# The first FFN's up product as seven half-size products of summed quarters, on one core

## The reference

```
def _ffn_sublayer(x, shift, scale, gate, pre_g, post_g, w_gu, w_down):
    h = _modulate(_rmsnorm(x, pre_g), shift, scale)
    a, b = jnp.split(h @ w_gu, 2, axis=-1)          # 1024 -> 2 x 2816
    y = (jax.nn.silu(a) * b) @ w_down               # 2816 -> 1024
    return x + FFN_RES_WEIGHT * gate * _rmsnorm(y, post_g)
```

## Time and profile before

| | |
|---|---|
| median of 3 runs | 1954.67 us (1954.18 to 1955.05) |
| span of the profiled execution | 1951.0 us (no other time of it is shown) |
| TensorE busy in the span | 1907.6 us |
| VectorE, ScalarE, GpSimd busy | 1031.5, 820.3, 297.9 us |
| up and down parts of the first FFN, from the third block | 57.79 to 540.66 us |

### The profile page before, as it was taken

How to read it: one execution, slowest core, us unless ns; L and a number is a source line. 1 busy time by engine, 2 the same in 40 slices (tenths; PEclk the granted TensorE clock), 3 DMA queues, 4 the chain that set the end, 5 groups by cost and what they waited for, 6 DMA issues and landing times.

```text
span 1951.0 us, 30914 instructions
## 1 busy us (share of the span) xinstructions
PE 1907.6 (98%) x11473; PEld 1757.5 (90%) x11473; DVE 1031.5 (53%) x1746; ACT 820.3 (42%) x1480; POOL 297.9 (15%) x274
## 2 busy tenths in 40 slices
PE   8999999999998999999999999999999999999997
PEld 5999999999997789999999999997888988888887
DVE  7655433443357665466667766676333543233336
ACT  6322222212247655566556655675222552222223
POOL 0000000000000220153455336540000000000000
PEclk9999999999999999999999999999999999999999
DMA  8333333334221430011111110111223412222232
GB/s 332 119 127 122 128 130 129 125 123 128 80 84 52 146 109 1 3 59 49 35 44 51 49 59 22 48 44 44 97 97 103 156 34 97 97 96 96 95 98 79
DMA packets 50130, 174.83 MB, mean 90 GB/s; under 512 B 6788, under 2 KB 8964, under 8 KB 49808
## 3 DMA queue, kind: packets, MB, share of 16 engines
q1 hardware_dynamic: 38720, 129.95, 20.0%
q0 software_dynamic: 11344, 43.97, 7.1%
HBM read 167.03 MB, written 4.24 MB: 88 GB/s over the span
## 4 chain that ended last, share of the span: by engine, by line
PE 86%; ACT 5%; DVE 5%; issue 2%; DMA 1%; SPq 0%; ACTq 0%; DVEq 0%
PE ps L1862 78%; PE ps L1866 4%; PE ps L2252 1%; PE ps L2176 1%; DMA raw<-W 1%; DVE d_os L1762 1%; DVE d_c L1630 1%; PE ps L2206 1%; ACT w_hi L568 1%; PE ps L2308 1%; DVE w_lo L1162 1%; ACT L981 0%; ACT d_t L966 0%; DVE m_prod L1416 0%; ACT c_u L669 0%
## 5 line engine op out<-in xcount | busy, mean ns | idle before, releaser
L568 ACT ACTIVATE w_hi<-raw 128x1024 fp32r<-128x1024 f32 x193 | 204.6, 1060 | 715.5 <-PE ps L1862 715.2
L1162 DVE TENSOR_TENSOR w_lo<-raw,w_hi 128x1024 fp32r<-128x1024 f32 (+1 forms) x193 | 235.1, 1218 | 405.3 <-ACT w_hi L568 405.1
L1862 PE MATMUL ps<-h_hi,w_hi 128*128 128x384 f32 (+2 forms) x1376 | 407.6, 354 | 7.3 <-DVE h_lo L1231 3.0
L1862 PE MATMUL ps<-h_lo,w_hi 128*128 128x384 f32 (+2 forms) x1376 | 403.4, 348 | 0.0
L1862 PE MATMUL ps<-h_hi,w_lo 128*128 128x384 f32 (+2 forms) x1376 | 394.4, 346 | 0.0
L1862 PEld LDWEIGHTS ps<-h_hi,w_hi 128*128 128x128 f32 x1376 | 248.3, 188 | 27.8 <-DVE h_lo L1231 6.6
L1862 PEld LDWEIGHTS ps<-h_hi,w_lo 128*128 128x128 f32 x1376 | 251.4, 188 | 13.5
L1862 PEld LDWEIGHTS ps<-h_lo,w_hi 128*128 128x128 f32 x1376 | 251.5, 188 | 12.9 <-issue 1.2
L1862 PE MATMUL ps<-f_hi,w_hi 128*128 128x512 f32 (+1 forms) x352 | 134.9, 383 | 3.2 <-ACT Y L1104 1.9
L1862 PE MATMUL ps<-g_hi,w_hi 128*128 128x384 f32 (+2 forms) x444 | 132.4, 345 | 2.3 <-DVE g_lo L1364 2.3
L1862 PE MATMUL ps<-f_hi,w_lo 128*128 128x512 f32 (+1 forms) x352 | 133.9, 380 | 0.0
(11 more groups left out here) (338 smaller groups left out, 3455.5 us busy)
## 6 DMA issues: line engine op xcount, KB each, us to landing
raw<-W SPq DMA_DIRECT2D x221, 512.0 KB, 3.4
w_mod<-WMOD POOLq DMA_DIRECT2D x56, 512.0 KB, 3.7
w_mod<-WMOD SPq DMA_DIRECT2D x12, 512.0 KB, 16.0
g_row<-g_rows POOLq DMA_DIRECT2D x8, 768.0 KB, 4.5
X<-XT SPq DMA_DIRECT2D x4, 768.0 KB, 6.9
a_sw<-i_n POOLq DMA_DIRECT2D x40, 64.0 KB, 1.9
w_first<-WMOD SPq DMA_DIRECT2D x4, 512.0 KB, 11.0
x_spill<-X POOLq DMA_DIRECT2D x1, 2048.0 KB, 8.5
```

What stands on the lines that cost most here:

```text
L568: a.activation(hi, src, ACT.Copy).then_inc(s("w_hi"), 1)
L1162: v.tensor_tensor(lo, src, hi.bitcast(F32), ALU.subtract).then_inc(s("w_split"), 1)
L1862: return pe.matmul(out, lhsT, rhs, start=start, stop=stop)
```

## The change

Twenty of the 22 pairs (all but the first two) are no longer computed as blocks. Take a pair as a 2 x 2 array: weight quarters by input half and by `a` or `b` (4 rows of 128 each), tokens by input half and by token half (384 columns). The product of two such arrays takes eight products of quarters, or seven with sums of quarters on both sides. The kernel now does seven, named `A11, A12, S2, S3, S1, A22, S4`, of 12 matmuls each (4 rows x 3 parts), and they add up in three PSUM banks, some of which are copied out between two products.

- GpSimd makes four sums of weight quarters (128x512) a pair, and, once, four sums of token quarters (128x1536) in place in `X`, which the norm now fills with `h`.
- ScalarE and VectorE round and split seven half blocks (128x512) a pair in place of two blocks (`u_hi`, `u_lo` count them), four slots deep.
- The end of a pair: ScalarE copies bank 0 to `pa` and later to `pb[0]`, bank 2 to `pb[1]`; VectorE adds the rest from PSUM (`p_sum`), ScalarE takes SiLU, VectorE multiplies (`gate`) and `gate_round`, `gate_low` follow.
- The chunks are 4, 4, 4, 4, 6 hidden blocks. Down parts of the first four go in groups of four output pairs, 192 matmuls in all for a chunk.
- The modulation passes stand at fixed places: eight behind the first blocks, three in each of the first 14 pairs, and 8, 8, 8 and 6 in the four down parts, of which `done` says how many behind each output pair. Their loads are issued by SP, between the weight loads. They write a bf16 product to SBUF.
- `X` is overwritten, so SP loads it again from memory behind the last product.
- `ffn1_last` runs rows 0 to 4 of its first two blocks before row 5 of either.
- Semaphores of the gates of the mixer are merged under new names.

```diff
+FCH1 = [4, 4, 4, 4, 6]
+A11, A12, S2, S3, S1, A22, S4 = range(7)
+MOD_FIRST = 8
+def product_passes(q, pos):
+    if pos not in (A11, S2, A22) or q >= 14:
+        return range(0)
...
+def down_passes(c, j):
+    n = MOD_FIRST + (14 + 20 * (c - 1) if c else 0) + 3 * len(pairs_in(c))
+    done = (0, 3, 6, 7, 8) if c < 3 else (0, 3, 6, 6, 6)
+    return range(n + done[j], n + done[j + 1])
@@ sync
+            def load_pair_next(q):
+                sp.wait_ge(s("u_lo"), product_slot(q, A22) + 1)
...
+            def load_unit_next(n):
+                u = n // 2 if n < 48 else n - 24
+                if (n < 48 and n % 2 == 0) or u + 2 >= N_MOD - N_MOD0:
+                    return
+                sp.wait_ge(s("mod_pass"), n + 3)
+                sp.dma_start(w_mod[:, u % 2], WMOD.rearrange("u p (k n) -> u p k n", k=KT)[N_MOD0 + u + 2]).then_inc(wmod_loaded[u % 2], 16)
...
+            for n in range(B_LAST1 + RING, B_LAST1 + 2 * RING):
+                load(n, n % RING)
+            sp.wait_ge(s("u_mm"), SLOTS)
+            sp.dma_start(X[:, :, 0:CTX], XTv[:, :, 0:CTX]).then_inc(s("x_loaded0"), 16)
+            sp.dma_start(X[:, :, CTX:T], XTv[:, :, CTX:T]).then_inc(s("x_loaded1"), 16)
@@ gpsimd
+            g.wait_ge(s("h_ready"), 4)
+            g.tensor_tensor(X[:, 0:4, 0:TH], X[:, 0:4, TH:T], X[:, 0:4, 0:TH], ALU.subtract).then_inc(s("t_add"), 1)
+            g.wait_ge(s("h_ready"), KT)
+            g.tensor_tensor(quarter(0, 1), quarter(1, 1), quarter(0, 1), ALU.subtract).then_inc(s("t_add"), 1)
...
+                if q:
+                    g.wait_ge(s("u_lo"), product_slot(q - 1, S1) + 1)
+                g.tensor_tensor(s1[:], b1, b2, ALU.add).then_inc(s("s_add"), 1)
+                g.wait_ge(s("s_add"), 4 * q + 1)
+                g.tensor_tensor(s2[:], s1[:], a1, ALU.subtract).then_inc(s("s_add"), 1)
+                g.tensor_tensor(s3[:], a1, b1, ALU.subtract).then_inc(s("s_add"), 1)
+                if q:
+                    g.wait_ge(s("u_lo"), product_slot(q - 1, S4) + 1)
+                g.wait_ge(s("s_add"), 4 * q + 2)
+                g.tensor_tensor(s4[:], a2, s2[:], ALU.subtract).then_inc(s("s_add"), 1)
@@ scalar
+                if pos == 2:
+                    a.wait_ge(s("u_mm"), n + 1)
+                    a.wait_ge(s("g_ready"), q + 3)
+                    a.activation(pb[:, 0], pair_bank(q, 0), ACT.Copy).then_inc(s("p_copy"), 1)
+                    a.wait_ge(s("p_sum"), 3 * q + 1)
+                    a.activation(pa_of(q)[:], pa_of(q)[:], ACT.Silu).then_inc(s("p_silu"), 1)
@@ vector
+            def after_product(q, pos):
+                n = product_slot(q, pos)
+                if pos == 1:
+                    v.wait_ge(s("u_mm"), n + 1)
+                    v.wait_ge(s("p_copy"), 3 * q + 1)
+                    v.tensor_tensor(pa_of(q)[:], pair_bank(q, 1), pa_of(q)[:], ALU.add).then_inc(s("p_sum"), 1)
+                    if q > first_pair(chunk_of(q)):
+                        gate_low(q - 1)
+                if pos == 4:
+                    v.wait_ge(s("u_mm"), n + 1)
+                    v.wait_ge(s("p_copy"), 3 * q + 3)
+                    v.tensor_tensor(pb[:, 1], pair_bank(q, 0), pb[:, 1], ALU.add).then_inc(s("p_sum"), 1)
+                if pos == 5:
+                    v.wait_ge(s("u_mm"), n + 1)
+                    v.tensor_tensor(pb[:, 0], pair_bank(q, 2), pb[:, 0], ALU.add).then_inc(s("p_sum"), 1)
+                lo_ahead(n, n + 1)
+                if pos == 5:
+                    gate(q, 0)
+                if pos == 0 and q > first_pair(chunk_of(q)):
+                    gate(q - 1, 1)
...
+                for m in product_passes(q, pos):
+                    mod_unit(m)
@@ tensor
+                for pos in range(7):
+                    pe.wait_ge(s("u_lo"), it * 36 + (n + pos + 1))
...
+                    if pos in (S2, S1, A22):
+                        pe.wait_ge(s("p_copy"), it * 12 + (3 * q + (S2, S1, A22).index(pos) + 1))
+                    if pos == S4:
+                        pe.wait_ge(s("p_sum"), it * 12 + (3 * q + 2))
+                    out_ = pair_bank(q, (0, 1, 0, 2, 0, 2, 0)[pos])
+                    for k in range(4):
+                        for i in range(3):
+                            last = pe.matmul(out_, slot_of((w_hi, w_hi, w_lo)[i], n + pos, k), (hi, lo, hi)[i][pos][:, k],
+                                             start=pos in (A11, A12, S3) and k == 0 and i == 0, stop=True, skip_group_check=True)
+                    last.then_inc(s("u_mm"), 1)
```

More of the change, by code:

```diff
@@ L444, in _ @@
+            for q in range(N_SEVEN):
+                weight_sums(q)
             g.wait_ge(s("mod_pass"), MOD_PASSES + 2)
@@ L1380, in down @@
                                 last.then_inc(psum_read[blk.pair], 1)
-                            if u0 is not None and c < 2:
-                                mod_unit(it, u0, j, int(c > 0))
                     if kind == "down" and c:
@@ new lines, in ffn1 @@
+            def ffn1():
+                gemm(Blk(B_FFN1, 0, 2), h_hi, h_lo, segs_even)
+                gemm(Blk(B_FFN1, 0, 3), h_hi, h_lo, segs_even)
+                for q in pairs_in(0):
+                    products(0, q, product_slot(q, 0))
+                down(0, 0)
+                with pe.Fori(0, 3, 1) as it:
+                    for q in pairs_in(1):
+                        products(it, q, product_slot(q, 0))
+                    down(it, 1)
+                for q in pairs_in(4):
+                    products(0, q, product_slot(q, 0))
+                pe.sem_inc(s("gemm_done"), B_LAST1 - 4)
+                ffn1_last()
@@ L2438, in _mod_units, with _ffn1_blocks @@
     return np.stack([tiles[u] if u < N_MOD0 and u % KT in MOD0_PE else rows[u] for u in range(N_MOD)])
+def _ffn1_blocks(w_gu, w_down):
+    gu = _tiles(w_gu)
+    out, hid = [], 0
+    for c, n in enumerate(FCH1):
+        pair = np.stack([gu[hid:hid + n], gu[HID + hid:HID + hid + n]], 1)
+        rows = w_down[hid * P:(hid + n) * P]
+        out += [pair.reshape(2 * n, P, D)]
+        out += [rows.reshape(n, P, 4, 2, P).transpose(2, 1, 3, 0, 4).reshape(4, P, D) if c < 4 else _tiles(rows)]
+        hid += n
+    return out
 def _ffn_blocks(w_gu, w_down):
```

493 lines of the change are left out of this document (393 added, 100 removed).

## The result

The changed kernel takes 1958.11 us (median of 12 runs, 1956.09 to 1960.34) against 1953.59 (12 runs, 1951.62 to 1955.05) of the kernel before beside it: ratio 1.0021, 95% interval 1.0014 to 1.0029. It is 4.5 us slower where 10 us less were forecast: inside the stated range of 1921 to 1961, but it moved the other way.

What follows compares the result with a forecast made beforehand. TensorE, busy 98%, was taken to bound the kernel: -41.6 (matmuls) +12 (pairs) +15.3 (start) +5 (down chunks) -0.4 (end) = -9.7, giving about 1945 us; stated range 1921 to 1961.

Steps and rivals of the forecast that it cites:

- 240 fewer matmuls at 0.1734: First FFN on TensorE: 2544 matmuls of 384 columns instead of 2784, at unchanged pace, -41.6 us.
- the rival of wait overhead: Waits before products: each costs TensorE 0.1 us, 14 us in all, total 1959; chance 0.05.
- the free port: Rival: VectorE tensor_tensors not held by GpSimd, or port shared by element; -32.8 us, total 1922; chance 0.22.
- The middle pairs: Pairs of chunks with passes: port waits cost 3.8 us in each of three chunks.
- the walk: Timed instruction order of a middle pair: TensorE waits 0.4 us for ScalarE's copy, 0.65 for the PSUM sum.
- A middle pair loses 1.1: Middle pair's walked loss, with 2.0 to 2.3 if GpSimd holds the port through two sums; 1.5 taken.
- one port carries 14.1 of 14.57 us: First 14 pairs: VectorE's instructions with two SBUF inputs and GpSimd's sums share one SBUF port, nearly filling a pair.
- The start: Norm to end of first pair: token sums and VectorE's late queue cost 15.3 us (bounds 11 and 18); 0.8 more in first chunk.
- the rival with full lengths: Held VectorE instructions cost their full row: 17.8 us at the start, 2.0 in each of 13 pairs, total 1961; chance 0.15.
- The down parts: Chunks 2 and 3: passes waiting for loads delay additions of Y, so TensorE waits; +5 us (bounds 2 and 8).
- The end: Behind the last product: shorter stall, but third block's weights late by 1.5 us; -0.4 us net.
- falls to about 1.1: End stall of 3.06 us shrinks to this because the fifth gated block's work is done first.

Runs made afterwards that it cites:

- 8: Changed kernel with passes moved out of the start and first pair, one per middle pair, more in down parts, token sums behind the norm: 1948.80 us, ratio 0.9976.
- 12: Changed kernel with one of a pair's three passes moved from behind the third product's place to behind the seventh's: 1950.64 us, ratio 0.9976.
- 13: 8 with two passes per middle pair at A22 and S4, 12, 9, 9 and 8 in down parts, weight sums on GpSimd: 1934.17 us, ratio 0.9896.
- 4: Changed kernel with GpSimd's weight sums cut to 32 of 512 columns in all pairs but the first and 15th: 1936.01 us, ratio 0.9906.
- 11: Changed kernel with the weight sums on VectorE alone, passes where they are: 1950.40 us, ratio 0.9983.
- 2: Changed kernel with GpSimd's four token sums cut to 32 of 1536 columns: 1947.16 us, ratio 0.9963.
- 5: Changed kernel with the first eight modulation passes put off to pairs 14 to 16 as the code counts them: 1955.62 us, ratio 1.0012.
- 3: Changed kernel with the modulation passes in the down parts cut to 32 of 1024 columns: 1950.68 us, ratio 0.9985.
- 6: Changed kernel with the down parts' modulation passes spread, one behind each addition of Y, two left out in chunk 3: 1950.17 us, ratio 0.9983.

## Why the prediction was wrong

**Right.** 240 fewer matmuls at 0.1734; the waits before products cost nothing where they are met (504 in one piece), so the rival of wait overhead falls; VectorE's tensor_tensors are held, so the free port falls; the two instructions at which TensorE waits in middle pairs, and none from pair 14 on; the waits for additions of Y in the third and fourth down part, three of them, with one in the second that was not forecast. Every mechanism of the forecast is in the trace, and one that it did not have, the clock. Four terms were too small, each by 1.6 to 4.4 us and all on the same side, 12 together: more than the 9.7 that were forecast as gain.

**The middle pairs (priced 11.4, measured 15.1).** The step that failed is the walk's times: "A middle pair loses 1.1", of which it then took 1.5, the middle of its bounds. The pair loses 2.04, 1.1 at the fifth product (walked 0.4) and 0.9 at the seventh (walked 0.65). Counted like the walk, from the end of the pair's first product (271.24), the first weight sum ends at 3.6 (walked 3.2), the pass at 4.65 (4.3), the low part at 6.6 (6.15), the copy at 7.2 (6.65) and the PSUM sum at 12.2 (11.5). On top, TensorE's first matmul starts 0.05 and 0.14 behind its releaser's end and the second 0.28 and 0.25 behind the first, which rows 2 and 3 could not show, since they have no wait. That the idle times, 0.85 and 0.66, add up to the 1.5 taken is luck: the walk counted starts. It also gave 0.8 to the last pair of a chunk and nothing to the first; it is the first that loses 0.8, and the last nothing.

And the walk was summed up as load ("one port carries 14.1 of 14.57 us"). Runs 8 and 12 show that it is the place of one pass: four products later it saves 0.9 a pair at equal load, and two passes in the idle stretch cost nothing (13). The loss also falls away without the weight sums (4), and by half with these on VectorE (11): both engines' work between the first and the seventh product makes the chain, and taking either engine's part out of it is enough.

**The start (priced 16.1 with pair 1, measured 18.5).** The step that failed is the walk from the norm to the first pair's third product, which was too short. The third block starts at 62.08 where the walk had 61.1 (0.4 of it in the norm, 3.4 for "3.0"), the fourth at 73.17 for 71.5, the third product at 89.09 for 86.15, the seventh at 105.20 for 102.25. So all that is missing, 2.9, is missing by the third product; pair 1 loses nothing where 0.8 was taken. VectorE works there almost without a gap, and its held instructions are long: passes of 4.51 and 4.33 beside the token sums, then a low part of 2.03 (0.96 alone), a token remainder of 2.83 (1.75) and a pass of 2.31 (1.24) beside the four weight sums, where the walk gave a token remainder 1.7 and named one weight sum. The prices of the rival with full lengths, 17.8 here and 2.0 a middle pair, were nearer, but not by its mechanism: the remainder shown above ends 0.55 behind its release and not 0.68. The start gives 8.8 back without the token sums (2) and 7.7 without the first eight passes (5), and would give 1.5 more in each without a fall of the clock on the chain; the combined kernel (8, with the first pair's passes gone too) gives 12.8. How the 2.9 divide among the held instructions stays open.

**The down parts (priced 5, measured 9.4).** The step: "the third needs a load issued after the first ends, 3.7 us to landing", counted for chunks 2 and 3 alone at about 2.2 each. The waits lose 1.2, 4.5 and 2.1, or 7.8, inside the bound of 8: chunk 1, whose units serve two passes, loses 1.2 too, and in chunk 2 the landings, 4.0 in the median where 3.7 was taken, hold the chain for up to 4.8 at a time, so that the third pass is later. The other 1.6 had no term at all: the forecast gave all 2544 matmuls the pace of a granted clock of 1.00, and behind the last of these waits TensorE ran at 0.50. Runs 3 and 6 confirm the mechanism of the waits: short or spread, the loss is gone or nearly so.

**The end (priced -0.4, measured +1.2).** The step: "falls to about 1.1". Eight pieces in a row, each of ScalarE or VectorE (a weight rounding and its remainder, the last gate, its rounding and low part, the clearing of `y_acc`, an addition of Y, the remainder of the third block), stand between the last product and 549.69; the 37 matmuls that `ffn1_last` can do meanwhile are 4.8 us of these 6.8. I had taken the fifth gated block's work as done first, and it is not: `pa_x` is there only at the end of the last product.

The range held the time. The chance of slower, 0.19, was too small: +32 stood against -41.6, and the two largest of these terms share one cause (what a hold costs VectorE's queue), so that their errors could be expected to add up and not to cancel.

## What to carry to other kernels

Sum the work on a shared port to see whether there is a problem, but walk the order to price it: what matters is what stands between two instructions that TensorE waits for, and moving one instruction by a few slots was worth 9 us. Each wait of TensorE costs some 0.2 us on top of its idle time, so count the waits as well, and look at the granted clock behind them: a stretch of 3 us at 0.50 cost 1.6 us wherever the chain ran through TensorE. Where GpSimd would only add two SBUF tensors beside a busy VectorE, VectorE does it for less: 0.68 us there against 1.6 to 2.1 on GpSimd and a held instruction on the other side.
